# The paired up projection of the last feed-forward layer: another order of the work on VectorE and ScalarE, and the halves of the gate's SiLU kept in PSUM

## What is computed

```python
def swiglu(x, w_gate, w_up, w_down):
    return (jax.nn.silu(x @ w_gate) * (x @ w_up)) @ w_down
...
        h = rms_norm(x, ffn2_norm[l])
        x = x + FFN_RESIDUAL_WEIGHT * swiglu(h, ffn2_w_gate[l], ffn2_w_up[l], ffn2_w_down[l])
    return rms_norm(x, final_norm)
```

## Time and profile before

| | us |
|---|---|
| device time, median of 3 runs | 2172.81 (2172.16 to 2173.91) |
| device time of the profiled execution | 2173.03 |
| its span, first to last instruction | 2171.2 |
| PE busy | 2131.9 (98%) |
| DVE busy | 1036.0 (48%) |
| ACT busy | 941.3 (43%) |
| POOL busy | 937.6 (43%) |

### The profile page before, as it was taken

One profiled execution on the slowest core, in us unless ns is written; L12 is line 12 of the kernel. 1 busy time (PEld: TensorE's weight loads), 2 busy tenths in 40 slices (PEclk: granted clock), 3 DMA queues, 4 the chain that ended last, 5 costly groups with the idle time before them and its releaser, 6 DMA issues.

```text
span 2171.2 us, 29176 instructions
## 1 busy us (share of the span) xinstructions
PE 2131.9 (98%) x11584; PEld 1779.4 (82%) x11584; DVE 1036.0 (48%) x1807; ACT 941.3 (43%) x1629; POOL 937.6 (43%) x437
## 2 busy tenths in 40 slices
PE   9999999999999999999999999999999999999898
PEld 8788877788888888888888888778888887999786
DVE  7684555437555402553331143735553139777511
ACT  7735555545444422442223233743265244444421
POOL 4423322344644444554444442144424445666432
PEclk9999999999999999999999999999999999999999
DMA  4213311332322322233323232133322222232221
GB/s 180 93 50 119 110 59 50 117 105 70 116 97 97 117 91 74 88 107 97 97 97 98 97 102 68 39 98 98 117 69 78 97 97 69 97 100 100 97 93 49
DMA packets 56439, 200.68 MB, mean 92 GB/s; under 512 B 6640, under 2 KB 7536, under 8 KB 55920
## 3 DMA queue, kind: packets, MB, share of 16 engines
q1 hardware_dynamic: 52416, 188.77, 26.4%
q10 hardware_dynamic: 3888, 10.05, 1.4%
HBM read 194.60 MB, written 2.10 MB: 91 GB/s over the span
## 4 chain that ended last, share of the span: by engine, by line
PE 89%; DVE 7%; ACT 2%; issue 1%; POOL 0%; ACTq 0%; DVEq 0%
PE dense L1015 14%; PE dense L1016 14%; PE dense L1017 14%; PE misc L1015 5%; PE misc L1016 5%; PE misc L1017 4%; PE misc L939 3%; PE misc L941 2%; PE misc L940 2%; PE dense L1037 1%; PE dense L998 1%; DVE misc L2587 1%; PE dense L988 1%; DVE a_kept L2663 1%; PE dense L1039 1%
## 5 line engine op out<-in xcount | busy, mean ns | idle before, releaser
L861 POOL TENSOR_TENSOR w_lo<-raw,w_hi 128x1024 fp32r<-128x1024 f32 x313 | 770.2, 2473 | 1024.8 <-ACT w_hi L1733 997.1
L1733 ACT ACTIVATE w_hi<-raw 128x1024 fp32r<-128x1024 f32 x316 | 326.9, 1051 | 147.0 <-PE dense L1017 84.7
L1015 PE MATMUL dense<-u_hi,w_hi 128*128 128x512 f32 x608 | 237.3, 390 | 0.0
L1017 PE MATMUL dense<-u_hi,w_lo 128*128 128x512 f32 x608 | 236.6, 389 | 0.0
L1016 PE MATMUL dense<-u_lo,w_hi 128*128 128x512 f32 x584 | 227.2, 389 | 0.0
L1015 PE MATMUL dense<-a_hi,w_hi 128*128 128x512 f32 x400 | 156.0, 390 | 0.0
L1016 PE MATMUL dense<-a_lo,w_hi 128*128 128x512 f32 x400 | 155.6, 389 | 0.0
L1017 PE MATMUL dense<-a_hi,w_lo 128*128 128x512 f32 x400 | 155.6, 389 | 0.0
L1015 PE MATMUL misc<-u_hi,w_hi 128*128 128x512 f32 x368 | 144.6, 393 | 3.7 <-DVE u_lo L2569 3.7
L1017 PE MATMUL misc<-u_hi,w_lo 128*128 128x512 f32 x368 | 144.0, 391 | 0.0
L1016 PE MATMUL misc<-u_lo,w_hi 128*128 128x512 f32 x360 | 141.1, 392 | 0.0
(11 more groups left out here) (565 smaller groups left out, 5030.2 us busy)
## 6 DMA issues: line engine op xcount, KB each, us to landing
raw<-in_weights SPq DMA_DIRECT2D x352, 512.0 KB, 3.5
h<-in_x SPq DMA_DIRECT2D x4, 512.0 KB, 6.6
alibi<-in_alibi ACTq DMA_DIRECT2D x1, 2048.0 KB, 8.2
h<-in_x ACTq DMA_DIRECT2D x2, 1024.0 KB, 7.4
out<-result SPq DMA_DIRECT2D x8, 256.0 KB, 2.2
p_raw<-in_p ACTq DMA_DIRECT2D x2, 512.0 KB, 3.4
hn<-mqk ACTq DMA_DIRECT2D x4, 256.0 KB, 4.0
mqk<-mqk ACTq DMA_DIRECT2D x4, 256.0 KB, 3.9
```

Source lines behind the costliest of these rows:

```text
L861: nc.gpsimd.tensor_tensor(w_lo[:, ring(s), :, :], raw[:, s % RAWS, :, :], w_hi[:, ring(s), :, :].bitcast(F32), ALU.subtract).then_inc(w_sp ...
L1015: mm(out, hi, x_hi, start=(i == 0), stop=False)
L1017: last = mm(out, lo, x_hi, start=False, stop=(i == k - 1))
L1733: f(w_hi[:, ring(s), :, :], raw[:, s % RAWS, :, :], ACT.Copy).then_inc(w_part, 1)
```

## The change

It leaves the matmuls and their order as they are, and changes the order around them and one place of storage:

- `rewrite_sums` (DVE): the eight `u_lo` come ahead of the four `s_all`; `rewrite_hi` (ACT): the four `s_hi` come after the eight `u_hi`. `s_hi` and `s_lo` become four tensors each; sum i has its high and low part side by side in 8 KB, over the place of four chunks of `a_lo`.
- In a pair, ACT rounds the weight blocks in the order 0, 2, 3, 1, 4, 6, 5 (before 0, 2, 1, 3, 5, 4, 6); block 0 of pair p + 2 already at the end of pair p.
- DVE multiplies the finished chunk right after the last sum, and only then starts on the weights of the next pair: `pair_one` and `pair_two` stand behind the first y sum, `pair_two_lo` and `pair_four` behind the second, `pair_four_lo` behind the z sum, `pair_one_lo` behind the next pair's multiplication.
- SiLU of the gate's halves goes to columns 256 to 511 of x and y, not to a slot; the multiplication becomes two instructions of 256 columns, each with one operand in PSUM. PE starts pair p + 2 on these banks when that multiplication is done.
- `a_lo` and `a_hi` of chunks 5 to 20 (`apart`) are spread over the last pair and what follows, by what has been freed.

```diff
+SUM_AT = (2, 0, 1, 3)
...
-        s_hi = arena("s_hi", 54, [4, 4, 256], F32R)
-        s_lo = arena("s_lo", 70, [4, 4, 256], F32R)
+        s_hi = [arena(f"s_hi{i}", 54 + 8 * q, [4, 256], F32R) for i, q in enumerate(SUM_AT)]
+        s_lo = [arena(f"s_lo{i}", 58 + 8 * q, [4, 256], F32R) for i, q in enumerate(SUM_AT)]
...
                     else:
-                        pe.wait_ge(st_act, 2 * (p - 2) + 1)
+                        pe.wait_ge(a_raw, FC * LAYER_OF[name] + c - 1)
                     product(p, 0, x, "a11", True)
                     pe.wait_ge(st_lo, 3 * p + 1)
                     if c == PAIRED[name][0]:
                         pe.wait_ge(st_slo, 4)
-                    if c >= PAIRED[name][0] + 2:
-                        pe.wait_ge(st_out, 5 * (p - 2) + 4)
                     product(p, 1, y, "s2", True)
...
                 for c in range(DC):
-                    if sums and c in (1, 2, 3, 4):
-                        sum_hi_of(name, c - 1)
...
                     f(u_hi[:, c, :], scaled[c % len(scaled)], ACT.Copy).then_inc(u_part, 1)
+                for i in range(4 if sums else 0):
+                    sum_hi_of(name, i)
...
-                    f(dst[:, 0:256], x, ACT.Silu).then_inc(st_act, 1)
+                    f(x[:, 256:S], x[:, 0:256], ACT.Silu).then_inc(st_act, 1)
                     if more:
-                        pair_four(p + 1)
+                        pair_two(p + 1)
                         pair_one(p + 1)
                         pair_raw(p + 1, 6)
+                        pair_four(p + 1)
                     else:
+                        act.wait_ge(st_used, BLOCKS * p + 4)
+                        apart(9, 13)
                         feed_to(rounded[0] + 1)
                     act.wait_ge(st_out, 5 * p + 4)
-                    f(dst[:, 256:S], dst[:, 256:S], ACT.Silu).then_inc(st_act, 1)
+                    f(y[:, 256:S], slot[c % 2][:, 256:S], ACT.Silu).then_inc(st_act, 1)
+                    if c + 2 < paired_to:
+                        pair_raw(p + 2, 0)
...
-                    TT(dst, slot[c % 2][:, :], slot[2 + c % 2][:, :], ALU.mult).then_inc(a_raw, 1)
+                    x, y, _ = (psum[b] for b in pair_banks(p))
+                    TT(dst[:, 0:256], x[:, 256:S], slot[2 + c % 2][:, 0:256], ALU.mult)
+                    TT(dst[:, 256:S], y[:, 256:S], slot[2 + c % 2][:, 256:S], ALU.mult).then_inc(a_raw, 1)
```

More of the change, by code:

```diff
@@ L819, in pair_pool @@
                 low(2, raw_half(p, 0, 1), 2)
-                low(3, three, 4)
-                low(6, raw_half(p, 1, 1), 7)
+                low(3, three, 3)
+                low(6, raw_half(p, 1, 1), 6)
             for s in range(NSLABS):
@@ L1029, in paired @@
                           "a22": (u_hi[:, 4:8, second], u_lo[:, 4:8, second])}
-                blocks.update({f"s{i + 1}": (s_hi[:, i, :, :], s_lo[:, i, :, :]) for i in range(4)})
+                blocks.update({f"s{i + 1}": (s_hi[i], s_lo[i]) for i in range(4)})
                 def product(p, i, out, a, start):
@@ L2558, in rewrite_sums @@
                     STT(u_all[:, c, :], h[:, c, :], V(gain, c), r_sb[:, :], ALU.mult, ALU.mult).then_inc(ux_done, 1)
+                for c in range(DC):
+                    dve.wait_ge(u_part, k0 + c + 1)
+                    TT(u_lo[:, c, :], u_all[:, c, :], u_hi[:, c, :].bitcast(F32), ALU.subtract).then_inc(u_ready, 1)
                 dve.wait_ge(ux_done, 3 * DC + 4)
@@ L2566, in rewrite_sums @@
                     TT(s_all[:, i, :, :], x, y, op).then_inc(st_diff, 1)
-                for c in range(DC):
-                    dve.wait_ge(u_part, k0 + c + 1)
-                    TT(u_lo[:, c, :], u_all[:, c, :], u_hi[:, c, :].bitcast(F32), ALU.subtract).then_inc(u_ready, 1)
             def sums_lo(name):
@@ L2647, in ffn_gate, with apart @@
                         pair_four_lo(p)
-                        pair_one_lo(p)
                 if paired_from == FC:
                     return
+                def apart(lo, hi):
+                    for c in range(lo, hi):
+                        dve.wait_ge(a_part, FC * n + c + 1)
+                        TT(a_hi[:, c, :], a_kept[:, c, :], a_lo[:, c, :].bitcast(F32), ALU.subtract).then_inc(a_ready, 1)
                 def last_out(c):
@@ L2670, in ffn_gate @@
                         last_out(c - 1)
-                    if more:
-                        pair_one(p + 1)
-                        pair_two(p + 1)
-                    if c > paired_from:
                         product(c - 1)
+                    pair_one_lo(p)
                     dve.wait_ge(st_used, BLOCKS * p + 2)
@@ L2679, in ffn_gate @@
                     if more:
-                        pair_two_lo(p + 1)
-                        pair_four(p + 1)
-                    if c - 1 < KEPT_FROM:
-                        low_a(c - 1, slot[(2 if c > paired_from else 0) + (c - 1) % 2])
+                        pair_one(p + 1)
+                        pair_two(p + 1)
+                    else:
+                        apart(5, 8)
                     dve.wait_ge(st_used, BLOCKS * p + 4)
```

71 lines of the change are left out of this document (42 added, 29 removed).

## The result

The changed kernel takes 2153.68 us (median; 2152.84 to 2154.06) against 2173.36 (2172.16 to 2174.46) for the kernel before on the same chip: 19.7 us less, a ratio of 0.9909 with a 95% interval of 0.9892 to 0.9926. The prediction was 2153.0, with a range of 2148 to 2160.

A forecast was written before the change was run, and what follows sets the result against it. PE, waiting on late DVE instructions, bounds the kernel: of 29.5 us lost, 0.9 + 3.9 + 2.0 + 1.6 + 0.4 + 0.6 = 9.4 stay, a gain of 20.1 from 2173.03, say 2153.0 us; range 2148 to 2160, about 0.8.

The forecast's parts named there:

- pool of 29.5 us: PE's loss against gapless matmuls: 6.4 us in groups 4 to 7, 13.4 in 18 pairs, 9.7 in `down2`'s first group.
- restarts: In the pairs, 0.4 us in all stays lost for PE's restart after each wait.
- Part 1: Groups 4 to 7: with `u_lo` ahead of the sums, PE waits 0.9 us instead of 3.9; 0.9 of 6.4 stays.
- The entry: First pair, product 1: PE newly waits 3.9 us for block 1's low part, then half clock costs 2 us.
- The table load: Before the first SiLU: 1.28 us without the skill's 1.38 us drain; with it, wait 5.3 us and time 2154.4.
- Part 2: Order in a pair: the y sum's 0.63 us wait in 16 pairs goes; z sum keeps 0.3 us slack.
- The first pairs' 1.6 us: First two pairs: low parts of chunks 3 and 4 delay the z sum, waits of 0.6 and 1.0 us.
- Part 3: `down2`'s first group: no `a_hi` wait, 9.7 us become 0.6; 2 return if the last low part meets two slabs.
- Pairs bound by DVE: Pairs: a late z sum costs 5.6 us (2158.6) or up to 11 us (2164); chance 0.14 for 2157.5 to 2166.
- The cheaper entry: Start of the pairs: clock does not fall and the chain is 2 us shorter, 2149 to 2147; chance 0.09.
- The slower case: Pairs: `pair_one` waits for POOL's whole run, each pair stands about 2.3 us, time 2190; chance 0.04.
- The clock: Start of the pairs: half clock decides 2 us; if it does not fall, 2151; chance 0.15 within the forecast's 0.70.

The follow-up runs named there:

- second profiled run: The changed kernel measured once more, nothing altered: median 2154.28 us (2153.03 to 2159.51), the profiled execution itself 2159.51 us.
- `a_hi` behind the sum: Changed kernel, with the two `a_hi` ahead of the last pair's last y sum on DVE moved after it: 2158.98 us.
- POOL behind `a_hi`: As `a_hi` behind the sum, with POOL's third and fourth slabs after the last pair held until `a_hi` of columns 16 and 20: 2153.26 us.
- sums first: Changed kernel, with the four sums ahead of the eight `u_lo` on DVE and `s_hi` among `u_hi` on ACT again: 2153.15 us.
- `s_lo` on POOL: Changed kernel, with three of the four `s_lo` (sums 1, 3 and 4) moved from DVE to POOL: 2149.86 us.
- copy first: On `s_lo` on POOL: first pair's copy of x ahead of two raw-weight casts, a low part behind the z and last y sums: 2148.15 us.
- PSUM only: Kernel before with its old order, only the SiLU halves in PSUM and the multiplication split in two: 2161.11 us, ratio 0.9944.
- split last: Changed kernel, with all `a_lo` and `a_hi` splitting of kept columns behind the last pair again: 2161.57 us, ratio 0.9947.
- order only: Changed kernel, with SiLU halves back in SBUF slots and one multiplication of 512 columns: 2155.91 us, ratio 0.992.

## Why the prediction was right, point by point

- **The bound and the pool of 29.5 us.** Left of it are 23.5 - 21.7 = 1.8, 190.0 - 181.4 = 8.6 and 0 us: 10.4, where the prediction had 9.4 (0.9, 7.9 and 0.6). That the total came within 1 us is in part luck, for inside the pairs two errors cancel: the waits were forecast at 6.1 (3.9, 1.6 and the last pair's 0.6) and are 4.6, while clock and restarts were forecast at 2.4 and took the other 4.0. In the second profiled run, without half clock, 1.3 stay in the pairs besides waits of 6.0, so the 0.4 for restarts was too small.
- **Part 1.** `u_lo` waited 0.7 for the 0.9 forecast. What the step left out: ACT's first SiLU, 3.3 us later now, also frees bank 0, for which group 6 waits 0.7 us. The prediction followed the moved SiLU down DVE's chain only, and not to the PSUM bank that it reads. Another 0.4 us lies in groups 4 to 7 themselves, which keep PE busy for 22.15 us instead of 21.7.
- **The entry.** The low part of block 1 was forecast for 1833.8 and ended at 1833.81. PE's wait was 2.8 in place of 3.9, because PE came later: the 0.7 at bank 0 and the slower groups had taken their share. Half clock came as forecast, and cost less than its length: with 6.8 us of it the pairs took 190.0, without it 188.6, 1.4 us for the 2.0 taken. Part of the slow time would have been waits anyway (1.1 and 1.0 for 0.6 and 0.3). With 3.4 us of it (`a_hi` behind the sum, POOL behind `a_hi`) the pairs took 188.62, no more than with none. That the sums' move is worth nothing follows from the prediction's own terms, 6.4 before and 0.9 + 3.9 + 2.0 after, and the run with the sums first shows it.
- **The table load.** The rows of the kernel after agree with the one read before: the load ends at 1817.82 and the SiLU starts at 1817.83. The 1.38 us drain that the Trainium skill names (ScalarE: Activation LUTs, "What ACT_TABLE_LOAD costs") is not seen here either, and the load placed early costs the later SiLU nothing.
- **Part 2.** Right in the mechanism and in the sentence that the order alone would do. The first pairs' 1.6 us came out as 0.7 and 0.3 for the z sum and 0.6 for the copy of x, so the size is luck: the z sum's waits were forecast at 1.0 and 0.6, and the wait for the copy was not named. ACT has two casts of raw weights ahead of that copy. Moving them behind it, and the low part behind the z sum, took 2.3 us from the pairs (185.64 to 183.35, the runs with `s_lo` on POOL without and with the copy first). Nor did the prediction name two waits of the first pair before, 1.2 us for POOL's low part (line 807) and 0.5 for the sum of line 2685; both stay with PSUM only and are gone wherever the new order stands, so these 1.7 us came back without a step of their own.
- **Part 3.** No wait for `a_hi`, and the last pair late by 0.3 for the 0.6 forecast. The step held in seven of eight runs by their times. Its warning named the wrong instruction: it is the last eight `a_hi` that can meet more slabs, and then 5 us return, not 2. The last low part took 2.90 us beside a slab in the changed kernel, and nobody waited for it.
- **The rivals.** Pairs bound by DVE: no, line 2711 ends at 1926.15 where PE's next product starts at 1926.69, a slack of 0.5 for 0.3. The cheaper entry: no, `s_lo` took 7.91 us where it had taken 7.92. The slower case did not come up in the pairs: `pair_one` met the last of POOL's instructions (it ended at 1922.29, and POOL then stood 3.0 us for ACT), so it had no run to let pass. Where POOL had several slabs queued, in the second profiled run from 2028.05 on, DVE got one `a_hi` in after each, as the prediction read it from the earlier trace rows. The clock was open to the end: it fell in one profiled run of the changed kernel and not in the other.

## What to carry to other kernels

Follow an instruction that you move to every one who waits for it, also to the buffer or bank that it frees: moving the sums here took 3 us from one wait and its half clock with it, and the time went to bank 0, to the low part of block 1, and to half clock behind that. When a stall is one late instruction, two remedies don't add up; try each alone before keeping both. And when an idle engine is let go earlier, look at what it will run beside.

## What the runs showed of the hardware

- The same wait of PE, 2.8 us at the same place, was followed by half clock (1.2 GHz) in one execution, with a mean of 0.50 over the 6.7 us from 1834.80, by a mean of 0.77 over the same stretch with the split last, and by full clock (2.4 GHz) throughout in the changed kernel's second profiled run. Six executions had this wait. Over the 10 us from its end the mean clock is 0.66 in the one where the wait ended earliest (1833.87), 0.83 in three (1834.07, 1834.07 and 1834.34), and 1.00 in the two where it ended latest (1835.36, and 1835.49 with the order only). An idle time of this length does not settle the clock by itself. That it also hangs on when the wait falls, as was put on record ahead of the second profiled run, fits these six; it is not shown, and what settles it is open.
- A run of DVE instructions with both operands in SBUF gets in about once per POOL instruction while POOL has more of them queued: eight `a_hi` took 13.67 us beside four slabs and 7.10 beside one. The Trainium skill (SBUF — State Buffer, "SBUF: two separate sides") describes the pair of ports that the two engines share as an exclusive lock for a whole instruction. The traces agree, and POOL pays too: in the second profiled run of the changed kernel the slab that two `a_hi` had slipped past took 3.38 us, the one before it, which held the `a_hi`, 2.41.
- The table for SiLU stays through copies: loaded at 1808.04, used at 1816.77 behind four casts, with no second load.
